# Pairs of weight units on TensorE: the 512-column matmuls of both units ahead of the 256-column ones

## The reference, cut to what matters

```python
def swiglu(x, w_gate, w_up, w_down):                      # first block
    return (jax.nn.silu(x @ w_gate) * (x @ w_up)) @ w_down
...
    gates = jax.nn.sigmoid(gate_logits.reshape(b, s, N_BRANCHES, D_MODEL))   # second block
    merged = gates[:, :, 0] * (y_a @ w_branch_a[layer]) + gates[:, :, 1] * (y_b @ w_branch_b[layer])
    x = x + merged @ w_out[layer]
    h2 = rms_norm(x, ffn_norm_g[layer])
    up = h2 @ w_up[layer]
    a, val = up[..., :D_FF_2], up[..., D_FF_2:]
    a = causal_depthwise_conv(a, conv_w[layer], conv_b[layer])
    x = x + (jax.nn.gelu(a, approximate=False) * val) @ w_down[layer]
```

## Time and profile before

| | us |
|---|---|
| median of 3 runs | 689.58 (689.29 to 689.66) |
| profiled execution, time | 689.52 |
| profiled execution, span from the first to the last instruction | 687.8 |
| TensorE busy in the span | 680.8 |
| VectorE busy | 482.7 |
| ScalarE busy | 416.9 |

### The profile page before, as it was taken

How to read it: one execution, slowest core, us unless ns; L and a number is a source line. 1 busy time by engine, 2 the same in 40 slices (tenths; PEclk the granted TensorE clock), 3 DMA queues, 4 the chain that set the end, 5 groups by cost and what they waited for, 6 DMA issues and landing times.

```text
span 687.8 us, 9420 instructions
## 1 busy us (share of the span) xinstructions
PE 680.8 (99%) x3784; PEld 586.9 (85%) x3784; DVE 482.7 (70%) x730; ACT 416.9 (61%) x706; POOL 91.2 (13%) x173
## 2 busy tenths in 40 slices
PE   9999999999999999999999999999999999999996
PEld 8888888888888888888888988888888888888885
DVE  6878796767666666667455767777868877777774
ACT  7787775755555555556555856665577755555553
POOL 3122020778200000012710000000000000000001
PEclk9999999999999999999999999999999999999999
DMA  9936534737555555536434336555453655555401
GB/s 343 386 133 230 199 122 155 280 126 244 184 187 192 202 196 197 189 131 218 177 148 154 123 123 213 197 191 179 160 212 135 228 201 184 183 187 187 178 1 61
DMA packets 19484, 126.13 MB, mean 183 GB/s; under 512 B 2416, under 2 KB 2544, under 8 KB 5232
## 3 DMA queue, kind: packets, MB, share of 16 engines
q1 hardware_dynamic: 19296, 125.34, 50.3%
q10 hardware_dynamic: 144, 0.20, 0.1%
HBM read 124.48 MB, written 1.05 MB: 183 GB/s over the span
## 4 chain that ended last, share of the span: by engine, by line
PE 99%; DVE 0%; issue 0%; ACT 0%; POOLq 0%; POOL 0%; ACTq 0%
PE bank L435 96%; PE bank L443 3%; DVE xres L1438 0%; POOLq L2121 0%; DVE last L1438 0%; ACT last L996 0%; ACT junk L993 0%; POOL ss L1932 0%; DVE ones L1465 0%; ACTq L145 0%
## 5 line engine op out<-in xcount | busy, mean ns | idle before, releaser
L1438 DVE TENSOR_TENSOR wlo<-raw,whi 128x1024 fp32r<-128x1024 f32 x222 | 270.5, 1230 | 61.5 <-ACT whi L996 58.1
L996 ACT ACTIVATE whi<-raw 128x1024 fp32r<-128x1024 f32 x222 | 230.4, 1052 | 5.8 <-PE bank L435 3.9
L435 PE MATMUL bank<-xb,whi 128*128 128x512 f32 x496 | 124.1, 392 | 0.0
L435 PE MATMUL bank<-xa,whi 128*128 128x512 f32 x432 | 108.2, 392 | 0.0
L435 PEld LDWEIGHTS bank<-xb,whi 128*128 128x128 f32 x496 | 90.4, 188 | 17.2
L435 PE MATMUL bank<-whi,xb 128*128 128x512 f32 (+1 forms) x352 | 96.2, 355 | 0.0
L435 PEld LDWEIGHTS bank<-xa,whi 128*128 128x128 f32 x432 | 78.9, 188 | 15.5
L435 PEld LDWEIGHTS bank<-xb,wlo 128*128 128x128 f32 x496 | 67.7, 190 | 4.9
L435 PEld LDWEIGHTS bank<-whi,xb 128*128 128x128 f32 x352 | 62.4, 190 | 9.0
L435 PE MATMUL bank<-whi,hh 128*128 128x512 f32 (+1 forms) x180 | 69.7, 387 | 0.0
L435 PE MATMUL bank<-wlo,hh 128*128 128x512 f32 (+1 forms) x180 | 69.6, 387 | 0.0
(11 more groups left out here) (246 smaller groups left out, 796.9 us busy)
## 6 DMA issues: line engine op xcount, KB each, us to landing
raw<-in_w_dram SPq DMA_DIRECT2D x109, 1024.0 KB, 4.8
first<-in_first_dram SPq DMA_DIRECT2D x8, 388.0 KB, 5.5
raw<-in_w_dram SPq DMA_DIRECT2D x4, 512.0 KB, 8.7
bias<-in_bias_dram SPq DMA_DIRECT2D x1, 1024.0 KB, 9.4
xres<-in_x_dram SPq DMA_DIRECT2D x1, 1024.0 KB, 8.1
gain<-in_ffn_norm_w_dram SPq DMA_DIRECT2D x1, 512.0 KB, 8.9
gain<-in_mix_norm_g_dram SPq DMA_DIRECT2D x1, 512.0 KB, 9.6
gain<-in_ffn_norm_g_dram SPq DMA_DIRECT2D x1, 512.0 KB, 5.0
```

Of the source, the lines that this page charges most:

```text
L435: return e.matmul(o, l, r, start=start, stop=stop)
L996: return e.activation(o, i, ACT.Copy, **options)
L1438: return e.tensor_tensor(out=o, in0=a, in1=b, op=op)
```

## The change

`feature_unit` is cut into `feature_high` (the 8 matmuls of 512 columns) and `feature_low` (the 8 of 256 columns). For a pair, gate and up in the feed-forward layers from f = 4 on and the two gates of the merge, TensorE now works high of the first unit, high of the second, low of the first, low of the second. The waits for the second unit's weights and bank move with its high part, ahead of the low part of the first. Single units keep their order. The lists of ACT, DVE, POOL and SP are unchanged.

```diff
-        def feature_unit(u, bank, x):
-            h, l = whi[u % NH], wlo[u % NH]
+        def feature_high(u, bank, x):
+            h = whi[u % NH]
             for k in range(KT):
                 mm(pb[bank][:, :], h[:, k * 128:k * 128 + 128], flat(x[:, k, :, :]), k == 0, False)
+
+        def feature_low(u, bank, x):
+            l = wlo[u % NH]
             for k in range(KT):
                 m = mm(pb[bank][:, 0:256], l[:, k * 128:k * 128 + 128], x[:, k, 0, :], False, k == KT - 1)
             return m
+
+        def feature_unit(u, bank, x):
+            feature_high(u, bank, x)
+            return feature_low(u, bank, x)
...
-                    feature_unit(u, bank, x).then_inc(*pe.done("free", u))
+                    feature_high(u, bank, x)
+                if what == "gu":
+                    w.wait_ge(*dve.of("lo", u + 1))
+                    w.wait_ge(*(dve.of("gate", n, 2 * (f - 4) + 1) if f < 6 else dve.of("up", n, f - 2)))
+                    feature_high(u + 1, bank + 1, x)
+                    feature_low(u, bank, x).then_inc(*pe.done("free", u))
+                    feature_low(u + 1, bank + 1, x).then_inc(*pe.done("free", u + 1))
+                elif what == "g":
+                    feature_low(u, bank, x).then_inc(*pe.done("free", u))
...
-                if what == "gu":
-                    w.wait_ge(*dve.of("lo", u + 1))
-                    w.wait_ge(*(dve.of("gate", n, 2 * (f - 4) + 1) if f < 6 else dve.of("up", n, f - 2)))
-                    feature_unit(u + 1, bank + 1, x).then_inc(*pe.done("free", u + 1))
...
                         w.wait_ge(*dve.of("gate sum", d - 1, b))
-                    feature_unit(u + b, b, xb).then_inc(*pe.done("free", u + b))
+                    feature_high(u + b, b, xb)
+                for b in range(2):
+                    feature_low(u + b, b, xb).then_inc(*pe.done("free", u + b))
```

## The result

The kernel with the change takes 691.82 us (median; 691.28 to 691.98) against 689.43 (688.93 to 689.82) for the kernel before, run beside it: 1.0034, with a 95% interval of 1.0023 to 1.0045. It is 2.4 us slower; 691.3 was forecast, and the range of 690.1 to 692.6 holds it. The profiled execution took 691.66 us, its span 689.9.

What follows compares the result with a forecast made beforehand. The prediction took TensorE to bound the kernel, busy 680.8 of 687.8 us. From the profiled 689.52, less 0.78 gain, plus stalls of 1.1, 1.27 and 0.2, it forecast 691.3 us, range 690.1 to 692.6.

Steps and rivals of the forecast that it cites:

- The gain on TensorE: One of two narrow-to-wide changes per pair goes: 0.02 us a pair, bounds 0 and 0.03; 0.78 us over 39 pairs.
- rival 3: Narrow matmuls behind longer wide runs come nearer to 0.11 than 0.12 us: up to 7 us, time 684 to 688; chance 0.03.
- Where the delay is hidden: Inside the layers the gate's copy comes 1.81 us later, but ACT's idle time covers it and everything behind shifts as a block.
- Rival 4: In the second layer late copies eat ACT's spare 1.76 us; each pair loses 0.05 or more, 692.2 and above; chance 0.06.
- End of the first layer: Up's join queues behind a split on DVE, the residual comes later, and TensorE's transposes wait 1.0 to 1.1 us; taken as 1.1.
- Start of the merge: Late joins in the first three pairs stall TensorE by 0.1, 0.85, 0.1 and 0.25 us; sum 1.27, gains included.
- the restart after a wait: TensorE's extra loss on starting again, 0 to 0.12 us each, 0 to 0.7 over some six waits; taken as 0.
- End of the second layer: The low half moves by 1.81 us to 674.95; the fourth held unit wants it at 674.78: a TensorE stall of 0.2.
- Rival 1: TensorE's order is worth nothing and the stalls are as worked out: 692.15 us; chance 0.08.
- Rival 2: One stall, at the first layer's end or the merge's second join, is covered; about 1.1 us falls away: 690.2; chance 0.13.

Runs made afterwards that it cites:

- split_later: Changed kernel, with DVE working the last of three splits behind the first layer after the residual's two additions, not ahead of them: 690.97 us, 1.0020.
- merge_head: Kernel before, with the new order only in the merge's first three pairs (d = 0 to 2): 690.79 us, 1.0021.
- four_runs: Kernel before, with each of 108 feature units worked as 4 wide, 4 narrow, 4 wide, 4 narrow matmuls: 691.63 us, 1.0032.
- covered_pairs: Kernel before, with the new order only in pairs f = 4 to 20 of both layers and d = 3 to 7 of the merge: 688.80 us, 0.9989.
- joins_first: Changed kernel; in merge pairs 0 and 1 both banks are copied and joined before the second unit's rounding and split, token product behind: 691.48 us, 1.0029.

## Why the prediction was right

**The gain on TensorE.** Forecast 0.02 a pair with a narrow run of 16 at 1.91 and wide runs of 3.6. Measured 1.91 and 3.63, 0.34 over 17 pairs of the first layer by the trace; 39 pairs gave 0.66 by time and 0.80 by the trace. The sum used 0.78.

In one reading the prediction is wrong: that the trace before has no run of 16 narrow matmuls. It has longer ones, in another form, where a group of units of the second block has outputs 256 columns wide. TensorE's timeline of the kernel before:

```profile
315.91 0.40 PE L435 MATMUL bank<-whi,xb 128*128 128x256 f32 x2
...
320.95 0.40 PE L435 MATMUL bank<-whi,xb 128*128 128x256 f32 x2
```

Between these two rows lie 14 rounds of three narrow matmuls, 0.36 a round, 0.12 each. This bears out the 0.96 for a second narrow run. It already spoke against rival 3 as well: these rows stand behind a long row of wide matmuls and still don't run nearer to 0.11.

The Trainium skill ("TensorE: Matmul & The Clock Gate", section "Back-to-back issue gap") has the distance of isolated matmuls hang on the columns alone, and says itself that in a real kernel's stream the weight loads help to set it. For this stream the columns alone do not do: 2.17 us lie between two orders of the same matmuls. The 256/2.4 + 2.5 = 109 ns of the formula is also short of the 1.91 / 16 = 0.119 us of the run of 16 narrow ones.

**Where the delay is hidden.** The gate's copy came 1.81 later, as worked out, and ACT's idle time ahead of it grew from 2.81 to 3.50: everything moved as a block. Rival 4 (each pair of the second layer loses) did not happen: from the first pair to the last it is 666.73 - 525.86 = 140.87 after and 665.12 - 523.90 = 141.22 before, start to start, so these pairs gain 0.02 each too; at that layer's end ACT still has 1.74 idle ahead of the gate's copy, where the earlier trace rows has 1.76. No wait shows in the middle of a layer.

**End of the first layer.** Forecast 1.1, by a join that has to queue behind a split and a chain with no gap up to the transposes. Measured 1.10, with the join at 293.00 straight behind the split, and split_later took it away where the theory said. It came in two parts, 0.82 ahead of the transposes and 0.28 among them, as they use the two halves of the weighing. The slack of about 0.1 that was read there saved nothing: the residual came 1.10 later, and TensorE lost 1.10.

**Start of the merge: the mechanism right, the size short.** The order of the stalls was right: the largest ahead of pair 1's second unit, small ones at the three other places. Forecast 1.27; measured 1.55 by the trace, 1.33 (0.8 to 2.1) by merge_head's time. The term that failed is the restart after a wait, bounded by 0 to 0.12 and taken as 0 on the ground that "the runs behind a wait are counted at 1.84 already". A run of eight that starts in 1.84 lasts 2.00; behind a wait it lasts 2.11, at 413.65 and again at 416.34. That is 0.11 for each of these two restarts. Pair 2's two lie inside one row (4.19 for 16) and can't be told from their stalls; at 0.11 too, the four make 0.44, and the bare stalls came out some 0.15 smaller than forecast. The upper bound of 0.12 would have been the better choice: it was the nearest row, and nothing in the trace spoke for 0.

**End of the second layer.** Forecast 0.2, measured 0.41. That the low half would be late by 0.2 was right: it ends at 676.58, and TensorE could have gone on at 676.15 + 0.23 = 676.38. But TensorE starts 0.14 after that end, and its next step takes 0.30 instead of 0.23. I count this as the same missing term, twice as large here; that it has the same cause is not shown.

**Sum.** With the measured terms: -0.66 + 1.10 + 1.55 + 0.41 = 2.40, against 2.39 by time. That the two meet to 0.01 is luck, as the interval of the time alone is 1.6 to 3.1; the trace's gain of 0.80 in place of 0.66 gives 2.26. The forecast was -0.78 + 1.1 + 1.27 + 0.2 = 1.79. Of the 0.6 between them 0.28 lies in the merge and 0.21 at the second layer's end, both put down to the restart term, which the range had taken in with 0 to 0.7. The rest, 0.12, is the gain that came out smaller by time.

**Rivals.** Rival 1 gave 692.15, which lies nearer to 691.82 than the forecast does, and for the wrong reason: it has no gain and no restart cost, and the two errors nearly cancel. The time alone would not have told them apart; four_runs and covered_pairs did. Rival 2 (a stall is covered) did not occur by itself, but its cover can be made, as split_later shows. Rival 3 (narrow runs faster than 0.95 for 8) did not occur: 1.91 for 16.

## What to carry to other kernels

When the order on the bounding engine changes, work out two things apart: what each instruction costs in its new neighbourhood, and how much later each result is handed over, followed along the other engines' lists to the next place where the list has no idle time left. A small gain in every round is easily lost at the few places where rounds end, so use the new order only where the late result is covered. And count a restart for each new wait: here eight wide matmuls behind a wait cost 0.11 us more than the same ones in a full queue.

## What was not expected of the hardware

- TensorE pays for a wait beyond the wait: the eight wide matmuls behind one last 2.11 us against 2.00, and behind the wait for `hl` the start comes 0.14 after the end of what it waited for, the next distance being 0.30 instead of 0.23. In the merge the start comes 0.05 after. Why these differ stays open. The first wide matmul behind the transposes of the earlier trace rows also lasts 0.48 instead of 0.39, and the next starts 0.31 behind it (302.18, 302.49), in the kernel before and with no wait shown; so it is not settled that a wait is the only cause.
- A change from narrow to wide matmuls costs 0.020 us by time, over 108 of them (four_runs). Which step of TensorE makes it was not tried.
- Moving one step on DVE brought a table load of 1.28 us on ACT onto the path (joins_first). The changed kernel has the same load, with ACT idle for 0.88 ahead of its next copy of a bank; there it costs nothing.
